# The first step of the expert loop, written out ahead of the loop in SyncE's program

## The chip, the cores and the metric

The kernel is one program on one core of a Trainium2 chip. Its five engines (TensorE or PE, VectorE or DVE, ScalarE or ACT, GpSimd or POOL, SyncE or SP) run their own instruction streams and meet at semaphores. SyncE computes nothing here: it issues nearly all transfers from HBM into SBUF. The metric is the device time of one execution, in microseconds (us), and its median over several runs.

## The reference

One denoising step of a small network: two layers over 128 context tokens and 128 latent tokens, width 1024, float32. Layer 0 mixes tokens by a two-way linear recurrence and a convolution, layer 1 by differential attention. After either mixer comes the part that the change touches, a mixture of experts on all 256 tokens:

```python
g_idx = jnp.argmax(g_logits, axis=-1)                      # one of 4 groups
e_in = jnp.take_along_axis(e_logits, g_idx[:, None, None], axis=1)[:, 0]
top_v, top_i = lax.top_k(e_in, TOP_K_INNER)                # 2 of its 8 experts
eid = g_idx[:, None] * EXPERTS_PER_GROUP + top_i
...
hid = jax.nn.silu(einsum('nd,edf->nef', hf, w_gate)) * einsum('nd,edf->nef', hf, w_up)
out = einsum('nef,efd->nd', hid * gates[..., None], w_down)
```

Each layer has 32 experts; an expert has 1024 x 256 gate and up weights and 256 x 1024 down weights. Which experts a token needs is known only after the router has run on the chip.

## The kernel before, in words

In each layer the router (PE and DVE) sorts the 512 pairs of token and expert by expert and cuts each expert's pairs into chunks of CH = 32 rows. The chunks are dealt to NC = 4 columns, one 32-wide strip of the PE array each, and the expert loop takes one chunk of every column per step. DVE writes the table of this into `meta`, a row of integers in SBUF: `meta[0]` is the number of steps (at most MAXS = 12), from M_EID on stand the expert numbers (four for each step), and from M_LOAD on four flags for each step, which say whether that column's expert is another one than in the step before. The flags of the first step are always 1. Then DVE raises the semaphore `meta0` (in layer 1 `meta1`; L1958), which SP, PE, ACT and DVE wait for.

SP then runs its own loop. It reads the number of steps into a register (L592). In each step it reads four expert numbers (L594) and four flags (L596), and then issues three sets of four transfers by L601: `gu0`, the first half of the gate and up weights of each column, `gu1`, the second half, and `down`. Each transfer is 128 partitions x 2048 floats, 1 MB, from an address that the expert number gives, into the buffer `EW` (program name `arena`), and it takes place only if its flag is 1. `EW` has one place for each column and part, so SP waits before each set until PE has done with it in the step before (`gu0_done`, `gu1_done`, `down`); PE raises all three once ahead of the loop, in its program before it waits for the last numbers of the table.

PE's loop does per step: the `gu0` matmuls (L1084, 32 of them), the `gu1` matmuls (L1084, 32 more), the gather of the next step's tokens (L1058), two transposes each at L1097 and L1100, the scatter of the previous step's result (L1069), and the `down` matmuls (L1112). The first gather (L1058) stands ahead of the loop; its result is copied into SBUF by ACT (L1395) and DVE (L2009), and the first `gu0` matmuls need these copies and the four `gu0` transfers. After the loop come two layer norms on DVE (the last at L1519 to L1545), the next layer, or the end.

Of the kernel before, what the change touches and what calls it, by code (L numbers as in the profile page):

```python
# [22 lines left out]
T = 128  # L23
NS = 2
# [11 lines left out]
NE = NG * EPG  # L36
FF = 256
CH = 32
NC = 4
MAXS = 12  # L40
GRID_W = 64
ROPE_BASE = 10000.0
LAM_INIT = 0.8 - 0.6 * float(np.exp(-0.3))
# [45 lines left out]
def rope_tables():  # L89
    nf = HD // 4  # L90
    inv = ROPE_BASE ** (-np.arange(nf, dtype=np.float64) / nf)
    tok = np.arange(T)
    pos = np.stack([tok // GRID_W, tok % GRID_W], 1)
    ang = pos[:, :, None] * inv[None, None, :]
# [79 lines left out]

M_EID, M_LOAD = 4, 4 + NC * MAXS
M_ALL = M_LOAD + NC * MAXS


def build(nc, a, o):
# [4 lines left out]
    def S(name):  # L184

        if name not in sems:
            sems[name] = ctx.enter_context(nc.semaphore(name))
        return sems[name]

    arena = ctx.enter_context(nc.sbuf_tensor("arena", [P, ARENA], F32))  # L190
    meta = ctx.enter_context(nc.sbuf_tensor("meta", [1, 1, M_ALL], I32))
# [3 lines left out]
    def region(n):  # L195
        at = top[0]
        top[0] += n
        assert top[0] <= ARENA, top[0]
        return at

    def view(at, n, pattern=None, **sizes):
        v = arena[:, at:at + n]
        return v.rearrange(pattern, **sizes) if pattern else v
# [16 lines left out]
    cond = view(region(KT * 32), KT * 32, "p (k n) -> p k n", k=KT)  # L220
# [7 lines left out]
    def sv(at, n, pattern=None, **sizes):  # L228
        assert at + n <= SCR, (at + n, SCR)
        return view(scr + at, n, pattern, **sizes)  # L230
# [20 lines left out]
    for c in range(6):  # L251
        n = min(4, 23 - 4 * c) * P
# [15 lines left out]
    for c in range(2):  # L268
        chunk(("out", 1, c), a["od_out_w"][c], 512, ("mix", 1, 1, c))
    at_chunk = {name: i for i, (name, *_) in enumerate(chunks)}  # L270
    ring_ld = [S(f"ring_loaded{i}") for i in range(3)]


    ASIDE = {("mod", 0, 3): 8192, ("evin", 0): 0, ("evin", 1): 4096}
    in_ring = [i for i, (name, *_) in enumerate(chunks) if name not in ASIDE]
    turn = {i: r for r, i in enumerate(in_ring)}

# [14 lines left out]
    def load_chunk(sp, i):  # L292
        name, src, cols, _ = chunks[i]
        if name in ASIDE:
            sp.dma_start(sv(PRE + ASIDE[name], 8 * cols), src).then_inc(S("loaded_" + "_".join(map(str, name))), 16)
            return
        r = turn[i]
        if r >= 3:
            BK.wait_filled(sp, chunks[in_ring[r - 3]][3])
        sp.dma_start(ring[:, r % 3, 0:8 * cols], src).then_inc(ring_ld[r % 3], 16)  # L300
# [213 lines left out]
    EW = sv(0, 4 * 6144, "p (b n) -> p b n", b=4)  # L514
# [21 lines left out]
    GU = [(0, 2048), (2048, 4096)]  # L536
    DN = (4096, 6144)
# [7 lines left out]
    def norm_no(l, w, s):  # L545
        return (l * 2 + w) * 2 + s
# [5 lines left out]
    def bias_dma(eng, n):  # L552

        l, c = MOD_ORDER[n]
        eng.dma_start(bias_at(n)[0:2, :], a["mod_b"][l:l + 1, c * 512:(c + 1) * 512].partition_broadcast(2))\
            .then_inc(S(f"ld_mbias{n % 3}" if n >= 4 else "ld_mbias_first"), 16)


    @block.sync
    def _(sp):  # L560
        sp.dma_start(condw[:, 32:48], a["cond"].rearrange("p k s -> p (k s)")).then_inc(S("ld_cond"), 16)
        load_chunk(sp, 0)
        sp.wait_ge(S("mbias_zero"), 2)
        for n in range(4):
            bias_dma(sp, n)
        sp.dma_start(cst, a["cst"]).then_inc(S("ld_cst"), 16)
        load_chunk(sp, 1)
        load_chunk(sp, 2)
        sp.dma_start(x[:, 0, :], a["x_prompt"]).then_inc(S("ld_x"), 16)
        sp.dma_start(x[:, 1, :], a["x_sample"]).then_inc(S("ld_x"), 16)  # L570
        load_chunk(sp, 3)
        sp.dma_start(vec, a["vec"]).then_inc(S("ld_vec"), 16)
        for i in range(4, 6):
            load_chunk(sp, i)
        sp.dma_start(wup, a["ev_w_up"]).then_inc(S("ld_up"), 16)
        sp.dma_start(aup, a["ev_a_up"]).then_inc(S("ld_up"), 16)
        sp.dma_start(gup, a["ev_g_up"]).then_inc(S("ld_up"), 16)
        for i in range(6, FIRST_OF_1 + 1):
            if i == 8:
                BK.wait_filled(sp, ("mod", 0, 3))  # L580
                sp.dma_start(S0, a["s0t"]).then_inc(S("ld_s0"), 16)
            load_chunk(sp, i)
        for l in range(2):

            BK.wait_filled(sp, ("mix", l, 1, 1))
            sp.dma_start(rw, a["r_w"][l].rearrange("p (k n) -> p k n", k=KT)).then_inc(S("ld_rw"), 16)

            sp.wait_ge(S("x_new"), norm_no(l, 0, 1) + 1)
            sp.wait_ge(S(f"meta{l}"), 1)
            if l == 1:  # L590
                sp.wait_ge(S("cache_out"), 32)
            steps = sp.value_load(meta[0:1, 0, 0:1], min_val=1, max_val=MAXS)  # L592
            with sp.Fori(0, steps) as it:
                expert = [sp.value_load(meta[0:1, 0, bass.ds(it * NC + (c + M_EID), 1)], min_val=0, max_val=NE - 1)  # L594
                          for c in range(NC)]
                fresh = [sp.value_load(meta[0:1, 0, bass.ds(it * NC + (c + M_LOAD), 1)], min_val=0, max_val=1)  # L596
                         for c in range(NC)]

                def load(part, lo, hi):
                    for c in range(NC):  # L600
                        sp.dma_start(EW[:, c, lo:hi],  # L601
                                     a["w_exp"][l, bass.ds(expert[c], 1), :, lo:hi].rearrange("e p n -> p (e n)"),
                                     cond=fresh[c]).then_inc(S(f"{part}_loaded{l}"), 16)

                for h, (lo, hi) in enumerate(GU):
                    sp.wait_ge(S(f"gu{h}_done{l}"), it + 1)
                    load(f"gu{h}", lo, hi)
                sp.wait_ge(S(f"down{l}"), it * 2 + 2)
                load("down", *DN)
            if l == 0:  # L610
                sp.wait_ge(S("x_new"), norm_no(0, 1, 1) + 1)
                sp.dma_start(CK, a["cache_k"]).then_inc(S("ld_cache"), 16)
                sp.dma_start(CV, a["cache_v"]).then_inc(S("ld_cache"), 16)
                for i in range(FIRST_OF_1 + 1, len(chunks)):
                    load_chunk(sp, i)
        for s in range(NS):
            sp.wait_ge(S("x_new"), norm_no(1, 1, s) + 1)
            sp.dma_start(o["y"][s], x[:, s, :]).then_inc(S("y_out"), 16)
        sp.wait_ge(S("y_out"), 32)
# [80 lines left out]
    def _(pe):  # L700
# [302 lines left out]
        def moe(l):  # L1003
# [71 lines left out]
            pe.wait_ge(S(f"meta{l}"), 1)  # L1075
            steps = pe.value_load(meta[0:1, 0, 0:1], min_val=1, max_val=MAXS)
            with pe.Fori(0, steps) as n:
# [127 lines left out]
    def _(act):  # L1205
# [169 lines left out]
        def moe(l):  # L1375
# [13 lines left out]
            act.wait_ge(S(f"meta{l}"), 1)  # L1389
            steps = act.value_load(meta[0:1, 0, 0:1], min_val=1, max_val=MAXS)  # L1390
            act.sem_inc(S(f"y_read{l}"), 1)
# [80 lines left out]
    def _(dve):  # L1472
# [386 lines left out]
        def moe(l):  # L1859
# [72 lines left out]
            own.link(TS(sc[:, 40:41], bank[:, 32:33], 1.0 / NC, None, ALU.mult))  # L1932
            own.link(TS(rv(R_KV, MAXS), cst[:, C_G4 + 12:C_G4 + 12 + MAXS], sc[:, 40:41], None, ALU.is_lt))
            own.link(V.tensor_reduce(sc[:, 48:49], rv(R_KV, MAXS), AX, ALU.add))
# [255 lines left out]
```

## Time and profile before

| | |
|---|---|
| runs | 1090.66, 1091.86, 1093.72 us; median 1091.86 us |
| profiled execution | 1089.75 us, of which the span of the profile is 1087.7 us |
| PE matmuls busy | 895.1 us (82% of the span) |
| DVE busy | 512.4 us (47%) |
| ACT busy | 171.2 us (16%) |
| mean granted TensorE clock | 0.887 of full speed |
| HBM to SBUF, queue of SP | 214.57 MB |

The profile gives the busy time of the engines, what each waited for, and a chain of work that ended last, followed back from the end of the program; what shortens a piece of that chain can shorten the program. Instructions of SP's own sequencer (reads of registers, arithmetic on them, issues of transfers) show as SPq. L592 is line 592 of the kernel before.

### The profile page before, as it was taken

How to read it: one execution, taken by the hardware profiler on the slowest of the kernel's cores; microseconds unless marked ns; L12 is line 12 of the kernel's file. 1: busy time of each engine (PE TensorE's matmuls, PEld its weight loads, DVE VectorE, ACT ScalarE, POOL GpSimd, SP SyncE). 2: the span in 40 equal slices, each digit the busy share in tenths (PEclk: the TensorE clock that was granted, in tenths of full speed). 3: DMA queues.
4: the chain of work that ended last, by engine and by line, in shares of the span. 5: the costliest groups of instructions: out<-in, count | busy, mean ns of one | idle time of the engine just before them, and what ended most of it. 6: DMA issues, size and time to landing. Idle time of an engine off the chain costs nothing.

```text
span 1087.7 us, 14397 instructions
## 1 busy us (share of the span) xinstructions
PE 895.1 (82%) x5288; PEld 545.2 (50%) x5288; DVE 512.4 (47%) x1212; ACT 171.2 (16%) x429; POOL 28.8 (3%) x56
## 2 busy tenths in 40 slices
PE   3899939999999997747998785999459658988983
PEld 1687826878778773533453332445334523533431
DVE  1248898676675755452242225110555532422335
ACT  0123211212111210200111002002330200110110
POOL 1000000000000000000000000000000000000000
PEclk9899959999998998867999897999569668999987
DMA  9901429555444401239689954642000267799980
GB/s 373 422 30 59 164 91 364 194 191 203 158 159 156 175 1 59 83 140 401 252 328 424 423 231 159 273 174 97 1 0 1 84 262 314 309 424 363 422 337 39
DMA packets 28778, 226.81 MB, mean 209 GB/s; under 512 B 4072, under 2 KB 4488, under 8 KB 7744
## 3 DMA queue, kind: packets, MB, share of 16 engines
q1 hardware_dynamic: 25216, 214.57, 49.3%
q0 software_dynamic: 3520, 11.66, 3.1%
q8 instruction: 28, 0.46, 0.2%
q14 instruction: 14, 0.11, 0.0%
HBM read 286.74 MB, written 2.39 MB: 266 GB/s over the span
## 4 chain that ended last, share of the span: by engine, by line
PE 62%; DMA 14%; DVE 13%; SPq 5%; issue 4%; ACT 2%; DVEq 0%; ACTq 0%
DMA arena<-in_w_exp 12%; PE ps L1128 8%; PE ps L1084 6%; PE ps L804 6%; PE ps L761 5%; PE ps L896 4%; PE ps L889 4%; PE ps L711 4%; PE ps L1069 4%; PE ps L1058 3%; PE ps L1112 3%; SPq L601 3%; PE ps L740 2%; DMA arena<-in_mod_w 2%; PE ps L731 1%
## 5 line engine op out<-in xcount | busy, mean ns | idle before, releaser
L1084 PE MATMUL ps<-arena 128*32 128x512 f32 x960 | 129.6, 693 | 56.2 <-DMA arena<-in_w_exp 56.1
L1084 PEld LDWEIGHTS ps<-arena 128*32 128x32 f32 x960 | 32.8, 125 | 149.3 <-issue 78.7
L2020 DVE TENSOR_SCALAR arena<-arena 128x256 f32<-128x256 f32 x15 | 4.4, 296 | 178.0 <-ACT arena L1400 178.0
L1128 PE MATMUL ps<-arena 128*128 128x512 f32 x192 | 85.1, 604 | 3.8 <-ACT arena L1222 3.8
L804 PE MATMUL ps<-arena 128*128 128x256 f32 x368 | 81.6, 380 | 2.3 <-ACT arena L1222 1.5
L1214 ACT ACTIVATE arena<-ps 128x512 f32<-128x512 f32 x74 | 44.0, 602 | 227.1 <-PE ps L889 135.2
L804 PEld LDWEIGHTS ps<-arena 128*128 128x128 f32 x368 | 69.0, 189 | 15.2 <-ACT arena L1222 1.9
L740 PE MATMUL ps<-arena 128*128 128x128 f32 x208 | 37.2, 336 | 40.0 <-DVE arena L2116 24.7
L1058 PEld LDWEIGHTS ps<-arena 128*128 128x128 f32 x544 | 62.1, 191 | 15.6 <-issue 13.3
L711 PE MATMUL ps<-arena 128*32 128x512 f32 x384 | 53.9, 667 | 18.7 <-DMA arena<-in_cst 12.8
L1058 PE MATMUL ps<-arena 128*128 128x128 f32 x544 | 65.1, 277 | 0.6 <-DVE arena L1988 0.6
L1069 PE MATMUL ps<-arena 128*128 128x512 f32 x136 | 61.4, 593 | 1.8 <-DVE arena L2033 1.8
L1128 PEld LDWEIGHTS ps<-arena 128*128 128x128 f32 x192 | 36.9, 193 | 50.9 <-issue 46.5
L761 PE MATMUL ps<-arena 128*128 128x512 f32 x128 | 59.7, 622 | 1.6 <-ACT arena L148 1.6
L896 PE MATMUL ps<-arena 128*128 128x192 f32 x320 | 60.0, 330 | 0.0
L889 PE MATMUL ps<-arena 128*128 128x128 f32 x384 | 56.8, 293 | 2.3 <-issue 2.3
L889 PEld LDWEIGHTS ps<-arena 128*128 128x128 f32 x384 | 49.0, 199 | 16.5 <-issue 14.9
L740 PEld LDWEIGHTS ps<-arena 128*128 128x128 f32 x208 | 31.1, 178 | 50.4 <-DVE arena L2116 28.0
L1112 PE MATMUL ps<-arena 128*32 128x512 f32 x480 | 54.6, 595 | 0.0
L896 PEld LDWEIGHTS ps<-arena 128*128 128x128 f32 x320 | 52.5, 194 | 0.0
L1811 DVE COPY arena<-ps 128x256 f32<-128x256 f32 x80 | 33.9, 424 | 37.3 <-PE ps L896 37.3
L1721 DVE SCALAR_TENSOR_TENSOR arena<-arena 128x256 f32<-128x256 f32 x120 | 51.4, 479 | 0.0
(296 smaller groups left out, 1049.4 us busy)
## 6 DMA issues: line engine op xcount, KB each, us to landing
arena<-in_w_exp SPq DMA_DIRECT2D x180, 1024.0 KB
arena<-in_mod_w SPq DMA_DIRECT2D x24, 2048.0 KB, 8.2
arena<-in_od_in_w SPq DMA_DIRECT2D x6, 2048.0 KB, 8.0
arena<-in_ev_in_w SPq DMA_DIRECT2D x5, 2048.0 KB, 28.0
arena<-in_ev_out_w SPq DMA_DIRECT2D x2, 2048.0 KB, 8.6
arena<-gate_rows POOLq DMA_DIRECT2D x8, 512.0 KB, 4.5
arena<-in_ln POOLq DMA_DIRECT2D x4, 1024.0 KB, 4.9
arena<-in_od_out_w SPq DMA_DIRECT2D x2, 2048.0 KB, 8.1
```

The costliest lines, as they stand in the source:

```text
L711: mm = pe.matmul(bank[q:q + 32, :], cond[:, k, :], w[:, k, :], start=(k < 4), stop=(k >= 4), skip_group_check=True)
L740: mm = pe.transpose(bank[:, n * P:(n + 1) * P], t, ident)
L761: mm = pe.matmul(BK.bank(key), hT[:, k, s * T:(s + 1) * T], slot(("out", l, n))[:, k, :], start=(k == 0), stop=(k == KT - 1))
L804: mm = pe.matmul(bank[:, n * 256:n * 256 + 256], slot(("evin", i // 4))[:, k, (i % 4) * P:(i % 4 + 1) * P], hT[:, k, :], start=(k == 0), s ...
L889: mm = pe.matmul(BK.bank(key)[:, i * P:(i + 1) * P], now[:, i, 0:P], lt[i], start=True, stop=True)
L896: mm = pe.matmul(BK.bank(key)[:, (i % 2) * 192:(i % 2) * 192 + 192], lt[i], now[:, i, :], start=True, stop=True)
L1058: mm = pe.matmul(ps[:, 4 + k // 4, (k % 4) * P:(k % 4 + 1) * P], hb[:, s, k * P:(k + 1) * P], sel[:, s, :], start=(s == 0), stop=(s == 1))
L1069: mm = pe.matmul(ps[:, 2 * s + half, :], tG[:, s * P:(s + 1) * P], ysb[:, half * 512:(half + 1) * 512], start=False, stop=last, skip_group ...
L1084: mm = pe.matmul(ps[32 * c:32 * c + 32, 6, :], xg[:, k, 32 * c:32 * c + 32], EW[:, c, k * 512:(k + 1) * 512], start=(k == 0), stop=(k == K ...
L1112: mm = pe.matmul(ps[32 * c:32 * c + 32, 4 + half, :], tH[:, f * P + 32 * c:f * P + 32 * c + 32], w, start=(f == 0), stop=(f == 1), skip_gr ...
L1128: mm = pe.matmul(BK.bank(key), hT[:, k, s * T:(s + 1) * T], slot(("odin", c))[:, k, :], start=(k == 0), stop=(k == KT - 1))
L1721: ins = STT(out, src, w, out, ALU.mult, ALU.add)
```

## The change

SP's first step is taken out of its loop. It waits for `gu1_done` and `down` once; then it reads the number of one expert and issues that column's `gu0` transfer, four times over, and issues the `gu1` and `down` sets behind them. These twelve transfers have no flag, and the four flags of the first step are not read. Then it reads the number of steps and runs the loop from step 1 on, which is as it was. The number of steps is declared to be at least MINS = 4 in SP's program. It is so for both layers. No other engine's program is changed.

```diff
+MINS = 2 * NS * T // (CH * NC)
...
-            steps = sp.value_load(meta[0:1, 0, 0:1], min_val=1, max_val=MAXS)
-            with sp.Fori(0, steps) as it:
+            def load(part, lo, hi, c, expert, **when):
+                sp.dma_start(EW[:, c, lo:hi], a["w_exp"][l, bass.ds(expert, 1), :, lo:hi].rearrange("e p n -> p (e n)"),
+                             **when).then_inc(S(f"{part}_loaded{l}"), 16)
+
+            sp.wait_ge(S(f"gu1_done{l}"), 1)
+            sp.wait_ge(S(f"down{l}"), 2)
+            first = []
+            for c in range(NC):
+                first.append(sp.value_load(meta[0:1, 0, M_EID + c:M_EID + c + 1], min_val=0, max_val=NE - 1))
+                load("gu0", *GU[0], c, first[c])
+            for c in range(NC):
+                load("gu1", *GU[1], c, first[c])
+            for c in range(NC):
+                load("down", *DN, c, first[c])
+            steps = sp.value_load(meta[0:1, 0, 0:1], min_val=MINS, max_val=MAXS)
+            with sp.Fori(1, steps) as it:
                 expert = [sp.value_load(meta[0:1, 0, bass.ds(it * NC + (c + M_EID), 1)], min_val=0, max_val=NE - 1)
                           for c in range(NC)]
                 fresh = [sp.value_load(meta[0:1, 0, bass.ds(it * NC + (c + M_LOAD), 1)], min_val=0, max_val=1)
                          for c in range(NC)]
 
-                def load(part, lo, hi):
+                for h in range(2):
+                    sp.wait_ge(S(f"gu{h}_done{l}"), it + 1)
                     for c in range(NC):
-                        sp.dma_start(EW[:, c, lo:hi],
-                                     a["w_exp"][l, bass.ds(expert[c], 1), :, lo:hi].rearrange("e p n -> p (e n)"),
-                                     cond=fresh[c]).then_inc(S(f"{part}_loaded{l}"), 16)
-
-                for h, (lo, hi) in enumerate(GU):
-                    sp.wait_ge(S(f"gu{h}_done{l}"), it + 1)
-                    load(f"gu{h}", lo, hi)
+                        load(f"gu{h}", *GU[h], c, expert[c], cond=fresh[c])
                 sp.wait_ge(S(f"down{l}"), it * 2 + 2)
-                load("down", *DN)
+                for c in range(NC):
+                    load("down", *DN, c, expert[c], cond=fresh[c])
```

The first place is where SP comes from the wait for `meta0` in layer 0. TENSOR_LOAD is a read of a number from SBUF, and ISA stands for arithmetic on registers. Before, the rows from there on are these:

```order
L592 TENSOR_LOAD meta [waits meta0,x_new]
L592 ISA x2
L593 UNCONDITIONAL_BRANCH
L593 ISA
L594 TENSOR_LOAD meta
L594 ISA x3
```

Three more reads by L594 and four by L596 follow, and the first transfer stands behind them:

```order
L596 TENSOR_LOAD meta
L596 ISA x2
L606 REGISTER_ALU
L601 ISA [waits gu0_done0]
L601 DMA arena<-in_w_exp 128x2048
```

Now the same place has one read ahead of the first transfer (L601 is now the read of an expert number and L594 the transfer):

```order
L601 TENSOR_LOAD meta [waits gu1_done0,down0,meta0,x_new]
L601 ISA x2
L594 ISA
L594 DMA arena<-in_w_exp 128x2048
L601 TENSOR_LOAD meta
```

Of the nine reads that stood ahead of the first transfer one is left: three expert numbers are now read between the first four transfers, the number of steps behind the twelfth, and the four flags of the first step not at all. The second place is SP's way from the last transfer of the first step into the loop, which is new:

```order
L594 DMA arena<-in_w_exp 128x2048
L607 TENSOR_LOAD meta
L607 ISA x2
L608 UNCONDITIONAL_BRANCH
L608 ISA
L609 TENSOR_LOAD meta
```

The read of the number of steps now stands there, behind twelve transfers. The rows of the loop's body, eight reads and twelve transfers, are the same as before but for their line numbers, and layer 1 has the same change.

## Rows read from the trace of the kernel before

**Rows 1.** The page's chain that ended last, shares of the span by engine and line

```profile
PE 62%; DMA 14%; DVE 13%; SPq 5%; issue 4%; ACT 2%; DVEq 0%; ACTq 0%
```

**Rows 2.** The chain, layer 0, in order: start us, us, what

```profile
470.95 0.07 DVE arena L1958
471.09 0.46 SPq L592
...
471.95 0.07 SPq L593
...
475.61 0.43 issue
...
477.67 0.16 SPq L601
...
477.93 0.36 SPq L601
```

**Rows 3.** The chain, layer 1, same columns

```profile
872.99 0.28 SPq L592
...
873.64 0.07 SPq L593
...
878.86 0.17 SPq L601
...
879.14 0.34 SPq L601
...
881.05 0.33 SPq L601
```

**Rows 4.** The timeline, both layers: start us, us, engine, line, [idle before <-releaser]

```profile
481.37 0.69 DVE L2009 COPY arena<-ps 128x512 f32<-128x512 f32 x1 [2.41 <-PE ps L1058]
...
492.27 6.23 PE L1084 MATMUL ps<-arena 128*32 128x512 f32 x32 [11.04 <-DMA arena<-in_w_exp]
...
882.89 0.69 DVE L2009 COPY arena<-ps 128x512 f32<-128x512 f32 x1 [2.26 <-PE ps L1058]
...
891.75 6.17 PE L1084 MATMUL ps<-arena 128*32 128x512 f32 x32 [8.99 <-DMA arena<-in_w_exp]
```

**Rows 5.** Stretches: length, busy of five engines, granted clock, DMA share, GB/s

```profile
474.00:476.00 2.00, 2.00 (x3) 0.67 (x2) 0.92 (x2) 0.00 (x0) 0.00 (x0) 0.50 0.00 0
...
478.00:480.00 2.00, 2.00 (x20) 2.00 (x20) 0.92 (x4) 0.52 (x1) 0.00 (x0) 1.00 0.53 106
...
482.00:484.00 2.00, 0.00 (x0) 0.00 (x0) 1.06 (x5) 0.00 (x0) 0.00 (x0) 0.97 0.90 311
...
488.00:490.00 2.00, 0.00 (x0) 0.00 (x0) 0.00 (x0) 0.00 (x0) 0.00 (x0) 0.50 0.99 418
...
880.00:882.00 2.00, 2.00 (x20) 2.00 (x19) 0.60 (x3) 0.60 (x1) 0.00 (x0) 1.00 0.97 283
882.00:884.00 2.00, 0.76 (x7) 0.57 (x6) 1.08 (x3) 0.00 (x0) 0.00 (x0) 1.00 1.02 426
```

**Rows 6.** The chain behind the first expert matmuls, both layers

```profile
483.62 18.55 DMA arena<-in_w_exp
502.21 6.38 PE ps L1084 x32
508.59 3.77 PE ps L1058 x32
...
519.81 6.88 PE ps L1084 x64
...
901.71 6.31 PE ps L1084 x32
...
919.24 6.88 PE ps L1084 x62
```

**Rows 7.** SP's loop ends, L593, layer 0, then layer 1: ns min/median/max, first and last start

```profile
L593 SPq ALU_OP  x7: 33/33/33, 487.1 to 628.4; - x7
...
L593 SPq ALU_OP  x8: 33/33/41, 887.7 to 1043.4; - x8
```

## The prediction

> **What bounds the kernel now.** I read the shares of the chain first [rows 1]. PE holds 62% of it, but 14% is waiting for transfers and 5% is SP's own sequencer, so what SP does one instruction at a time can set the end. The chain in order of time shows where. When DVE has raised the flag at 470.95 us, nothing else is on the chain but SP's reads until its first transfer at 477.93 [rows 2]; in layer 1 the same stretch runs from 872.99 to 879.14 [rows 3]. Then I asked the timeline what waits for these transfers. PE stands idle 11.04 us in layer 0 and 8.99 us in layer 1 ahead of its first expert matmuls, released by a transfer both times [rows 4]. The stretches show that the DMA engines have nothing to do meanwhile (share 0.00 at 474 to 476) and run at 418 GB/s once they are going [rows 5]. So both layers have a stretch in which DMA waits for SP and PE waits for DMA. Behind it the chain waits for the `gu1` transfers (until 502.21) and then goes from one PE line to the next through the first two steps [rows 6]. Nothing in it is fixed in time: each piece is released by the one before, so a start that is earlier by some time moves the rest by as much.
>
> **The change part by part.** *The reads ahead of the first transfer.* Before, SP reads the number of steps from 471.09 to 471.95, then enters the loop and reads four experts and four flags until the address arithmetic of the first transfer at 477.67. What stands between 471.95 and 477.67, 5.72 us, is gone from ahead of the first transfer, for the first expert number takes the place of the number of steps: same kind of read, two register instructions behind it, as the order shows [rows 2]. In layer 1 it is 878.86 less 873.64, 5.22 us [rows 3]. The two layers differ by 0.5 us mostly because of a hole of 0.43 us at 475.61 that layer 1 lacks; I take each as it was. Sum 10.94 us.
>
> *Two waits added ahead* (`gu1_done` and `down`, where `gu0_done` alone stood later). In PE's program they are raised ahead of PE's own wait for the table, so they are up when SP comes; what is left is the instruction. The trace has no wait that is satisfied at once with its gaps measured apart; the step from DVE's flag to the first read, 470.95 to 471.09, is 0.14 us and holds such a wait [rows 2]. I take 0.1 us a layer, with ends 0 and 0.28. Minus 0.2 us in all.
>
> *Three reads between the first four transfers.* They delay the second to the fourth transfer. A read with its register instructions took 0.86 us in layer 0 (471.09 to 471.95) and 0.65 us in layer 1, so three take 2.6 or 2.0 us. From SP's first issue to the fourth it took 1.9 us in layer 1 [rows 3]; it will be some 4. A transfer of 1 MB takes 2.5 us at 418 GB/s [rows 5], so the DMA engines come to the fourth only 7.5 us behind the start. I take nothing; the upper end is the three reads in full, 4.6 us for both layers.
>
> *The flags.* The first step's transfers took place before as well, since its flags are 1. No byte is saved. A transfer without a flag has as many instructions as one with it.
>
> *The number of steps, and the loop's first reads, now behind twelve issues.* When does SP come to the second step? Twelve issues took 9.2 us in layer 0 (477.93 to 487.1) and 8.6 us in layer 1 [rows 7]. To that come three reads (2.6, then 2.0), the number of steps (0.9, then 0.7) and the entry with eight reads (5.7, then 5.2). From a first transfer at 472.3 that is 490.7 in layer 0, and from 874.0 it is 890.5 in layer 1. What it must not miss is the end of the first `gu0` matmuls, now 492.27 + 6.23 = 498.5, then 492.9; in layer 1 891.75 + 6.17 = 897.9, then 892.8 [rows 4]. So the cover is 2.2 and 2.3 us: nothing is paid, and if the cover were gone, SP's next set would start late by what is missing, which costs only once its data is late for the second step (rival D).
>
> *PE's side of the wait.* The copy of the gathered tokens ends at 481.37 + 0.69 = 482.1 and 883.6. The transfers would let PE start at 492.27 less 5.6 = 486.7, and 891.75 less 5.1 = 886.6 [rows 4]. The copies are earlier by 4.6 and 3.0 us, so DMA is still what ends the wait, and the whole gain arrives. Were it not so, the gain would stop at the copy.
>
> **Sum:** 10.94 - 0.2 = 10.7 us, 5.6 in layer 0 and 5.1 in layer 1. Against the profiled execution, 1089.75, that is 1079.0 us; that execution lies 2.1 us under the median of the runs, 1091.86, and from the median it is **1081.2 us**.
>
> The read of a number takes 0.46 us in layer 0 and 0.28 in layer 1 [rows 2, 3]. The Trainium skill (DMA: Bandwidth & Descriptors, Latency and other measured facts) gives a floor of about 600 ns for it. By that floor the one read that is left would be longer by 0.14 and 0.32 us and the gain 10.2 us in place of 10.7; the trace has it shorter, and the sum goes by the trace.
>
> **How fast the transfers get going** is the largest unknown of size. From SP's first issue to PE's first expert matmul it is 14.3 us in layer 0 and 12.6 us in layer 1 for the same 4 MB [rows 2 to 4], because in layer 0 the engines are counted as busy at 0.90 yet move only 311 GB/s at 482 to 484, where layer 1 moves 426 two to four microseconds after its first transfer [rows 5]. I see no cause in the trace. If it hangs on the moment and not on the kernel, layer 0 may gain 1.7 us more, or layer 1 1.7 us less: 9.0 to 12.4 us in place of 10.7.
>
> **The clock of PE.** It was granted half speed (1.2 GHz) while PE was idle ahead of the expert matmuls [rows 5], and the first `gu1` matmuls took 6.38 and 6.31 us where 64 matmuls took 6.88 at 2.4 GHz [rows 6], which is 3.44 for 32. The idle time gets shorter, and if that kept the clock up, the chain would gain up to 2.9 us a layer more. Against it: a wait ahead of `gu1` remains, and a `gu0` done sooner makes that one longer. I take no gain.
>
> **The rivals.** *A. More than the sum:* the clock comes back earlier in both layers; 10.7 + 5.8 = 16.5 us at most, 1075.4. *B. Hidden anyway:* something other than SP's issue decides when the data lands, so that the stretch is filled by a slow start of DMA; 1091.9. For it speaks that layer 0 needs 1.7 us more for the same bytes; against it that the DMA engines stand at share 0.00 all the way until SP issues. The Trainium skill (DMA: Bandwidth & Descriptors, Issuing engines are not separate DMA queues) says that the sequencer's time to start a transfer is usually small beside the transfer. It would make this rival the likely one; here eight reads stand ahead of the start, 5 to 6 us of them, and no transfer runs beside them. *C. Part of it is given back:* layer 1 starts slowly too and the waits and reads cost their upper ends (0.6 and 4.6 us, of which I took 0.2): 10.7 - 1.7 - 5.0 = 4.0 us, 1087.9. *D. Slower:* SP's program has become longer, and SP must now get at the loop's instructions while 12 MB of transfers are under way, where before it entered the loop with DMA idle. If it stood still there until these twelve have landed (12.6 MB at 418 GB/s is 30 us, so until some 504 in layer 0 and 906 in layer 1), then reads took 6 us and the next `gu0` 12.6 us, it would land at 522 and 924. PE wants it at 519.81 - 5.6 = 514.2 and 919.24 - 5.1 = 914.1 [rows 6]. It costs 8 and 10 us, the whole is 7 us slower, 1099. It decides once the stop is beyond 16 us: about 11 us are covered (490.7 against 514.2 less 12.6), and 5.4 a layer are the gain. The only hole seen is 0.43 us [rows 2].
>
> **How the numbers follow.** About 0.3%, 3.3 us, is what can be told from no change. The forecast, a gain of 8.5 to 13 us, gets 0.66; A (13 to 17 us) 0.12; C (3.3 to 8.5 us) 0.13; B 0.06; D 0.03. The likeliest case's own range is 1078.9 to 1083.4. With half of A and half of C taken in, and for the 3 us by which the runs of before differ among themselves, the range is 1076.5 to 1085.5. Faster by over 0.3%: 0.91; within: 0.06; slower: 0.03.
>
> **What would show it.** In the trace of after, SP's first expert transfer comes 1.0 to 1.2 us behind the flag (before 7.0), PE's idle time ahead of the first expert matmuls is 5 to 6 us in layer 0 and 3.5 to 4 in layer 1, both still released by a transfer, and the distance from the first transfer to the first matmul stays between 12.6 and 14.3 us. SP's first transfer of the second step comes right behind the end of the first `gu0` matmuls and not behind SP's reads. The prediction is wrong if DMA starts early and the data lands as before, if PE is released by the copies, or if SP comes late to the second step.

## The result, and the profile after

| | before | changed |
|---|---|---|
| runs of the first comparison | 1091.26 us median of 4 (1089.07 to 1093.72) | 1076.37 us median of 4 (1069.36 to 1081.01) |
| ratio, 95% interval | | 0.9857 (0.9819 to 0.9895) |
| first repeat | 1091.93 (25 runs) | 1081.37 (6 runs), ratio 0.9885 (0.9847 to 0.9923) |
| second repeat | 1090.3 (11 runs) | 1079.05 (6 runs), ratio 0.9899 (0.9858 to 0.9940) |
| profiled execution | 1089.75 us, span 1087.7 | 1081.01 us, span 1078.9 |

The change makes the kernel faster by 1.0 to 1.4%. The first median, 1076.4 us, lies 4.8 us under the forecast of 1081.2 and just outside its range (from 1076.5); both repeats lie inside it, 0.2 us over and 2.2 us under the forecast.

The chain of the changed kernel, layer 0 (start us, us, what; L1969 is DVE's flag, L601 the read of an expert number, L594 a transfer of experts). It answers to [rows 2]:

```profile
474.72 0.07 DVE arena L1969
...
474.86 0.47 SPq L601
...
475.84 0.35 SPq L594
...
476.23 0.28 SPq L601
...
476.95 0.34 SPq L594
...
478.05 0.33 SPq L594
...
479.14 0.34 SPq L594
...
479.56 0.43 issue
```

And layer 1, which answers to [rows 3]:

```profile
869.82 0.07 DVE arena L1969
...
869.96 0.28 SPq L601
...
870.72 0.34 SPq L594
...
874.45 0.33 SPq L594
```

The first transfer now comes 1.12 and 0.90 us behind the flag, where it came 6.98 and 6.28 us behind it: 5.86 + 5.38 = 11.2 us. The hole of 0.43 us that stood among the reads of layer 0 is still there, at 479.56, but now behind the first four transfers, where it costs nothing. Layer 1, which had none before, now has one of 0.36 us at 872.96, between its second and third transfer.

The timeline, PE's first expert matmuls (L1095) and DVE's copy (L2020), both layers, as in [rows 4]:

```profile
485.16 0.69 DVE L2020 COPY arena<-ps 128x512 f32<-128x512 f32 x1 [2.42 <-PE ps L1069]
489.47 6.12 PE L1095 MATMUL ps<-arena 128*32 128x512 f32 x32 [4.45 <-DMA arena<-in_w_exp]
...
879.86 0.69 DVE L2020 COPY arena<-ps 128x512 f32<-128x512 f32 x1 [2.27 <-PE ps L1069]
884.25 5.01 PE L1095 MATMUL ps<-arena 128*32 128x512 f32 x32 [4.52 <-DMA arena<-in_w_exp]
894.19 5.16 PE L1095 MATMUL ps<-arena 128*32 128x512 f32 x32 [4.93 <-DMA arena<-in_w_exp]
```

PE's idle time has gone from 11.04 to 4.45 us and from 8.99 to 4.52, and a transfer still ends it, 3.6 and 3.7 us after the copy. Behind it the chain has the pieces of [rows 6]:

```profile
482.03 17.34 DMA arena<-in_w_exp
499.37 0.04 issue
499.41 6.27 PE ps L1095 x32
505.68 3.77 PE ps L1069 x32
...
516.89 3.42 PE ps L1095 x29
```

One way of adding up the profile serves for all that follows. The span is cut into five parts: up to DVE's flag in layer 0; from there to the end of the first `gu1` matmuls (stretch 0); on to the flag in layer 1 (middle); to the end of the first `gu1` matmuls there (stretch 1); and the tail. Each number is a difference of starts and ends in the timeline. For before, stretch 0 is 502.21 + 6.38 - 470.95 = 37.64 us. The flag of layer 1 before is this row of its chain:

```profile
872.86 0.07 DVE arena L1958
```

| profile | up to flag 0 | stretch 0 | middle | stretch 1 | tail |
|---|---|---|---|---|---|
| before | 470.95 | 37.64 | 364.27 | 35.16 | 179.68 |
| changed | 474.72 | 30.96 | 364.14 | 29.53 | 179.55 |
| changed, repeat 1 | 473.17 | 30.99 | 364.14 | 31.82 | 180.58 |
| changed, repeat 2 | 475.83 | 31.53 | 364.12 | 31.83 | 179.49 |

Middle and tail are the same to about 1 us, as the argument needs that a start earlier by some time moves the rest by as much. The two stretches sum to 72.8 us before and to 60.5, 62.8 and 63.4 after, on average 62.2: 10.6 us less, against 10.7 forecast. By layer the forecast is less close: layer 0 gained 6.1 to 6.7 us against 5.6, layer 1 gained 5.6, 3.3 and 3.3 against 5.1. What does not fit is the first 470 us, which in these four profiles differ by 4.9 us though their programs are equal.

### The profile page after: what moved, and what is told of

Same layout as the page of the kernel before. It is cut to its first block, busy times and chain, and to the rows that moved or that the text cites. A ratio compares the mean times of both kernels' runs of the same rounds, so it can differ in the third digit from the quotient of the medians.

```text
span 1078.9 us, 14351 instructions
## 1 busy us (share of the span) xinstructions
PE 895.7 (83%) x5288; PEld 548.5 (51%) x5288; DVE 512.4 (47%) x1212; ACT 170.8 (16%) x429; POOL 28.8 (3%) x56
## 4 chain that ended last, share of the span: by engine, by line
PE 62%; DMA 14%; DVE 13%; SPq 5%; issue 3%; ACT 2%; DVEq 0%; ACTq 0%
DMA arena<-in_w_exp 12%; PE ps L1139 8%; PE ps L1095 6%; PE ps L815 6%; PE ps L772 6%; PE ps L907 5%; PE ps L900 4%; PE ps L722 4%; PE ps L1080 4%; PE ps L1069 3%; PE ps L1123 3%; SPq L594 3%; DMA arena<-in_mod_w 2%; PE ps L751 2%; ACT arena L1233 1%
## 5 line engine op out<-in xcount | busy, mean ns | idle before, releaser
L1095 PE MATMUL ps<-arena 128*32 128x512 f32 x960 | 126.7, 679 | 46.5 <-DMA arena<-in_w_exp 46.3
L1095 PEld LDWEIGHTS ps<-arena 128*32 128x32 f32 x960 | 32.5, 123 | 137.4 <-issue 76.3
L815 PEld LDWEIGHTS ps<-arena 128*128 128x128 f32 x368 | 70.4, 193 | 15.6 <-ACT arena L1233 1.9
L1069 PEld LDWEIGHTS ps<-arena 128*128 128x128 f32 x544 | 62.1, 192 | 15.1 <-issue 12.9
L722 PE MATMUL ps<-arena 128*32 128x512 f32 x384 | 53.5, 662 | 18.9 <-DMA arena<-in_cst 12.8
L1139 PEld LDWEIGHTS ps<-arena 128*128 128x128 f32 x192 | 37.0, 194 | 50.9 <-issue 46.5
L900 PEld LDWEIGHTS ps<-arena 128*128 128x128 f32 x384 | 49.8, 202 | 15.8 <-issue 13.3
L751 PEld LDWEIGHTS ps<-arena 128*128 128x128 f32 x208 | 30.6, 176 | 50.4 <-DVE arena L2127 28.1
L1123 PE MATMUL ps<-arena 128*32 128x512 f32 x480 | 54.6, 595 | 0.0
L907 PEld LDWEIGHTS ps<-arena 128*128 128x128 f32 x320 | 54.5, 200 | 0.0
```

The costliest lines, as they stand in the source:

```text
L722: mm = pe.matmul(bank[q:q + 32, :], cond[:, k, :], w[:, k, :], start=(k < 4), stop=(k >= 4), skip_group_check=True)
L751: mm = pe.transpose(bank[:, n * P:(n + 1) * P], t, ident)
L815: mm = pe.matmul(bank[:, n * 256:n * 256 + 256], slot(("evin", i // 4))[:, k, (i % 4) * P:(i % 4 + 1) * P], hT[:, k, :], start=(k == 0), s ...
L900: mm = pe.matmul(BK.bank(key)[:, i * P:(i + 1) * P], now[:, i, 0:P], lt[i], start=True, stop=True)
L907: mm = pe.matmul(BK.bank(key)[:, (i % 2) * 192:(i % 2) * 192 + 192], lt[i], now[:, i, :], start=True, stop=True)
L1069: mm = pe.matmul(ps[:, 4 + k // 4, (k % 4) * P:(k % 4 + 1) * P], hb[:, s, k * P:(k + 1) * P], sel[:, s, :], start=(s == 0), stop=(s == 1))
```

## The experiments

All are edits of the changed kernel. *first* is its list of expert numbers of the first step. The arrival times at the first transfer are from the timelines: start of SP's first transfer less start of DVE's flag.

**The changed kernel again, twice.** No edit.

> The changed kernel itself, timed against the kernel before in five rounds, and profiled a second time. Theory 1, SP's reads: all of the gain lies between DVE's flag and SP's first expert transfer. In the trace the first transfer comes 1.1 us behind the flag in layer 0 and 0.9 in layer 1, where it was 7.0 and 6.3, so 11.3 us, and the time is 1079 to 1081 if the run before is at 1091 (ratio 0.989 to 0.990). Theory 2, the clock adds: PE is granted its full clock for longer behind the shorter waits, some 3 to 4 us more than the reads account for, ratio 0.985 to 0.987, and the stretch from the flag to the end of the first gu1 matmuls is shorter by over 12 us in sum. Theory 3, what the profiled pair shows outside the two stretches (3.8 us in the first 470 us, where the programs are equal) is chance: it has another size or sign in this profile.

> The changed kernel once more, five rounds, for its size. If the first four runs (median 1076.4) were a chance draw of a wide scatter: ratio between 0.987 and 0.991, and in the trace the two stretches from DVE's flag to the end of the first gu1 matmuls sum to 60 to 63 us (72.8 before), with the time ahead of the first flag somewhere in 470 to 478 us. If the change gives more than its stretches: ratio 0.986 or lower and a middle part (between the two stretches) under 363.5 us.

Ratios 0.9885 and 0.9899, medians 1081.37 and 1079.05 us. The first transfer came 1.12 and 0.90 us behind the flag in all three profiles. The stretches are in the table above. Theory 1 holds for the place of the gain: the repeats' stretches are shorter by 10.0 and 9.4 us, where theory 2 asked for over 12 (the first profile had 12.3). The 63.4 us of the second repeat lie a little above its expected 60 to 63; its middle, 364.12, is not the shorter one that its rival asked for. Theory 3 holds as well: the time up to the first flag was 474.7, 473.2 and 475.8 us in the three profiles of this kernel, and in all twelve profiles of the study it lies between 470.1 and 477.5 without any order that follows the edits. The view by stretches says what differs, here for the shortest and the longest of them, `four_first` and `nine_first`, whose programs are equal up to there:

```profile
0.00:470.09 470.09, 404.52 (x2547) 309.34 (x2547) 293.74 (x674) 89.02 (x209) 22.98 (x45) 0.92 0.44 167
```

```profile
0.00:477.46 477.46, 414.40 (x2547) 314.39 (x2547) 293.71 (x673) 89.17 (x209) 23.04 (x45) 0.90 0.43 164
```

The columns are length, then busy time of PE, PE's weight loads, DVE, ACT and POOL with their instructions, the granted clock, DMA share and GB/s. The same 2547 matmuls keep PE busy for 9.9 us more at a mean clock of 0.90 than at 0.92, and DVE, ACT and DMA do the same work in the same time. So the scatter in this part is PE's clock: how long it is granted 1.2 GHz in a stretch differs from one execution to the next. The runs without a profile agree. Over the 48 runs of the kernel before that the three later comparisons hold, the time falls by about 8.5 us for each 0.01 of mean granted clock (correlation -0.84), and over the 16 runs of the changed kernel by 9.5 us (-0.80). The slowest of the 48 had the lowest clock (0.879, 1099.4 us), and the fastest of the 16 the highest (0.902, 1069.4 us).

**All nine reads ahead of the first transfer again** (`nine_first`), the step still outside the loop, with its flags.

```diff
-            first = []
-            for c in range(NC):
-                first.append(sp.value_load(meta[..., M_EID + c:M_EID + c + 1], ...))
-                load("gu0", *GU[0], c, first[c])
...
-            steps = sp.value_load(meta[0:1, 0, 0:1], ...)
+            steps = sp.value_load(meta[0:1, 0, 0:1], ...)
+            first = [sp.value_load(meta[..., M_EID + c:M_EID + c + 1], ...) for c in range(NC)]
+            flag = [sp.value_load(meta[..., M_LOAD + c:M_LOAD + c + 1], ...) for c in range(NC)]
+            for c in range(NC):
+                load("gu0", *GU[0], c, first[c], cond=flag[c])       # and so for gu1 and down
```

> The first step stays ahead of the loop, but all nine reads stand in front of its first transfer as before (the number of steps, four experts, four flags), and the transfers have their flags. Theory 1: the nine reads at 0.5 to 0.65 us put the first transfer at 5 to 6 us behind the flag; only the address arithmetic of the reads and the loop entry are saved, so it is faster than the kernel before by 1 to 3 us and slower than the changed one by 8 to 10 (ratio 0.997 to 0.999). The rival, that a step ahead of the loop or a transfer without a flag is what gained: the ratio stays at 0.986 to 0.990.

Ratio 0.9963 (0.9936 to 0.9990), 1088.2 us. Its chain shows the reads back on it (L599 to L601):

```profile
477.46 0.07 DVE arena L1969
...
477.61 0.47 SPq L599
...
478.42 0.27 SPq L600
...
480.63 0.27 SPq L601
...
482.56 0.44 issue
...
483.56 0.36 SPq L594
```

The first transfer came 6.10 and 5.81 us behind the flag, the stretches sum to 69.0 us. Most of the gain is gone though the step is still outside the loop, so it was the reads. At the first transfer 1.35 us are left of it: the loop entry and the address arithmetic of reads with a counter, less a hole of 0.36 us that this kernel has among its reads in layer 1. The time came out a little better than expected, 3.7 us under before and 7 to 9 over the changed kernel. The stretches are 3.8 us shorter than before; beyond the 1.35 us that is a faster start of the transfers (1.2 us) and first `gu1` matmuls that took 5.05 us in layer 1 in place of 6.31.

**The flags kept** (`flags_kept`): each of the four columns reads its flag behind its expert number, and all twelve transfers have theirs.

```diff
                 first.append(sp.value_load(meta[..., M_EID + c:M_EID + c + 1], ...))
-                load("gu0", *GU[0], c, first[c])
+                flag.append(sp.value_load(meta[..., M_LOAD + c:M_LOAD + c + 1], ...))
+                load("gu0", *GU[0], c, first[c], cond=flag[c])
```

> As the changed kernel, but each of the first four columns has its flag read behind its expert number, and all twelve transfers have their flags. Theory 1: one read more ahead of the first transfer, 0.5 us a layer, so 1.0 to 1.3 us slower than the changed kernel; the first four transfers are 1.7 us apart, still under the 2.5 us that one takes to move. The rival, that the transfers without flags start or move faster: the distance from the first transfer to the first expert matmul grows again to 12.6 to 14.3 us, and the loss is 3 us or more.

Ratio 0.9916 (0.9892 to 0.9939), 1082.9 us. First transfer at 1.80 and 1.96 us, 0.7 and 1.1 us later than in the changed kernel; from there to the first expert matmul 14.56 and 13.45 us, about what the changed kernel's profiles show (13.5 to 14.8). The stretches sum to 64.3 us, 2.0 more than the changed kernel's mean. So a transfer without a flag is not seen to get going faster; the flags cost their reads, some 1.7 us together.

**Four reads, then four transfers** (`four_first`).

```diff
-            first = []
+            first = [sp.value_load(meta[..., M_EID + c:M_EID + c + 1], ...) for c in range(NC)]
             for c in range(NC):
-                first.append(sp.value_load(meta[..., M_EID + c:M_EID + c + 1], ...))
                 load("gu0", *GU[0], c, first[c])
```

> As the changed kernel, but the four expert numbers are read in one go ahead of the first transfer, which the four transfers then follow as fast as SP can issue. Theory 1: the first transfer comes 1.6 to 2.0 us later in each layer, so it is 3.2 to 4 us slower than the changed kernel. If transfers that follow each other fast reach full rate sooner than ones that are 1.1 us apart, a part of it comes back: the distance from the first transfer to the first gu1 matmul is then under the 23.5 us that the changed kernel's trace shows in both layers.

Ratio 0.9912 (0.9878 to 0.9946), 1082.0 us. The first transfer came 2.78 and 2.58 us behind the flag, 3.3 us later in sum than in the changed kernel. But to the first expert matmul it was then 13.64 and 12.74 us only, and to the first `gu1` matmul 23.5 and 22.7, where the changed kernel's three profiles have 24.1 and 24.3 on average. The stretches sum to 63.3 us, 1.1 us more than the changed kernel's mean and not the 3.2 to 4 of theory 1. What gives two thirds back shows in the rates. These are the first 10 us behind the first transfer in layer 1, in `four_first`:

```profile
868.17:878.17 10.00, 6.68 (x38) 4.55 (x36) 5.71 (x19) 0.60 (x1) 0.00 (x0) 0.95 0.91 353
```

in `before`, whose four follow each other 0.64 us apart in this layer:

```profile
879.14:889.14 10.00, 3.62 (x32) 3.43 (x31) 3.15 (x11) 0.60 (x1) 0.00 (x0) 0.88 0.92 360
```

and in the changed kernel, with two stretches of it:

```profile
870.72:872.72 2.00, 2.00 (x4) 0.86 (x3) 1.72 (x9) 0.00 (x0) 0.00 (x0) 0.50 0.54 94
...
874.72:876.72 2.00, 1.39 (x9) 0.83 (x8) 1.85 (x9) 0.00 (x0) 0.00 (x0) 1.00 1.00 365
...
870.72:880.72 10.00, 8.39 (x40) 5.24 (x38) 6.32 (x24) 0.60 (x1) 0.00 (x0) 0.87 0.90 329
```

The first 2 us are alike in all three (94 to 111 GB/s). The difference lies at 4 to 8 us behind the first transfer, where the DMA engines count as busy in all (share 0.90 to 1.03). They move 418 to 434 GB/s there in the three profiles without reads between the transfers, and 287 to 377 in seven of the nine with reads between them; `both` (381 and 418) and `warm` (422 and 397) lie higher. Over 10 us it is 329 against 353 and 360 GB/s in the rows shown, so about 0.3 MB or 0.7 us. PE does nearly the same work in `four_first` as in the changed kernel (38 and 40 matmuls in these 10 us), so it is not PE's work beside them.

Layer 0 of the kernel before looks like an exception, for it has no reads between its transfers and yet starts slowly. Its chain shows that its transfers do not follow each other closely either, since the issues of the second and the third took long:

```profile
478.58 0.99 SPq L601
479.85 0.74 SPq L601
```

From the first to the fourth transfer it takes 2.9 us there, where layer 1 takes 1.9. Sorted by that distance, all 24 bursts (twelve profiles, two layers) fall into two groups. Five have it at 1.6 to 2.0 us (`nine_first` and `four_first` in both layers, before in layer 1) and move 353 to 360 GB/s over their first 10 us; nineteen have it at 2.9 us or more and move 308 to 351. To the first expert matmul the five take 12.3 to 12.7 us in layer 1 and 13.5 and 13.6 in layer 0, the others 13.1 to 14.8 in layer 1 and 13.6 to 14.9 in layer 0. On average the others are 1.3 us later in layer 1 and 0.9 in layer 0. That the distance is the cause is argued and not shown: it was changed together with the moment of the first transfer, and a slow issue may be a sign of slow DMA engines as well as its cause.

**More reads behind the twelve transfers** (`late_reads`: 8, `late_many`: 32).

The edit of `late_many`:

```diff
+            for c in range(8 * NC):
+                sp.value_load(meta[0:1, 0, M_EID + c:M_EID + c + 1], min_val=0, max_val=NE - 1)
             with sp.Fori(1, steps) as it:
```

> As the changed kernel, with eight reads more (not used) behind the read of the number of steps, 4.4 to 5 us a layer. In the changed kernel's trace SP is ready for its second step 5.3 us before the first gu0 matmuls end in layer 0 and 2.8 us in layer 1. Theory 1, the prediction's cover: the reads eat it, SP's transfers for the second step come up to 2 us late in layer 1, and nothing is lost, since their data is wanted only some 11 us later than the latest issue in time; the same time as the changed kernel within 1 us. The rival, that the length of SP's program or its arrival at the loop matters by itself: slower by the added time, 5 to 10 us.

> As the changed kernel, with 32 reads more behind the read of the number of steps, 17 to 19 us a layer. Theory 1: SP comes some 12 to 16 us late to its second step; the data of the second step is then late by 1 to 8 us a layer, so 3 to 14 us slower than the changed kernel in sum, and PE has an idle time ahead of the second step's gu0 matmuls, released by a transfer, which it does not have in the changed kernel. If the slack of about 11 us that the prediction worked out is larger than thought, nothing is lost.

`late_reads`: ratio 0.9912 (0.9877 to 0.9947), 1081.1 us, as expected no loss to be seen (stretches 63.2 us, middle 364.1). `late_many`: 0.9916 (0.9885 to 0.9947), 1080.4 us, and here 3 to 14 us of loss were expected. SP came to its second step 12 and 15 us late (the first `gu0` matmuls ended at 492.3 and 885.3, SP was ready at 504.5 and 900.5). PE's timeline for the second step, first layer 0, then layer 1:

```profile
513.05 7.06 PE L1097 MATMUL ps<-arena 128*32 128x512 f32 x64
...
906.80 3.65 PE L1097 MATMUL ps<-arena 128*32 128x512 f32 x32 [0.22 <-DMA arena<-in_w_exp]
910.84 1.50 PE L1097 MATMUL ps<-arena 128*32 128x512 f32 x12 [0.40 <-DMA arena<-in_w_exp]
```

PE waits for the second step's data not at all in layer 0 and 0.6 us in layer 1. The middle part, which holds the second step of layer 0, is 364.0 us, as in the changed kernel, and the tail 178.9. The reason is in the durations of SP's transfers of that step (least, median, longest in ns):

```profile
L594 SPq DMA_DIRECT2D arena<-in_w_exp x12: 73/73/348, 504.8 to 514.6; - x12
```

An issue that moves data takes 333 ns or more; most of these take 73. Their flags are 0: in the second step most columns keep their expert, so there is far less than 12 MB to move and far more slack than the 11 us that were worked out from four transfers of a set.

**PE kept busy in the wait** (`warm`): five matmuls between the first gather and PE's loop.

```diff
             gather(0)
+            for n in range(5):
+                pe.matmul(ps[:, 7, :], ident, cst[:, 0:512], start=True, stop=True, skip_group_check=True)
```

> As the changed kernel, with five matmuls of 128x512 more on PE (into a PSUM bank that the first step does not use yet, result not used) between the first gather and the expert loop, about 4.3 us at 2.4 GHz. They fill the idle time ahead of the first gu0 matmuls. The theory that the clock sets a part of the gain: with the clock kept up the gu0 matmuls take 3.4 us in place of 5 to 6. By the prediction's reasoning the wait ahead of gu1 grows by the same 2 to 3 us, since the gu1 data sets its end, and the time stays that of the changed kernel within 1.5 us (longer wait, clock falls again). The rival: the clock stays up through gu1 as well, 2 to 3 us a layer faster.

Its timeline in layer 0, where L1087 is the added matmuls:

```profile
480.32 4.46 PE L1087 MATMUL ps<-arena 128*128 128x512 f32 x10
486.15 3.65 PE L1097 MATMUL ps<-arena 128*32 128x512 f32 x32 [1.37 <-DMA arena<-in_w_exp]
496.08 5.67 PE L1097 MATMUL ps<-arena 128*32 128x512 f32 x32 [6.28 <-DMA arena<-in_w_exp]
```

The first set takes 3.65 us in place of 6.12, the wait behind it is 6.28 us in place of 3.8, and the `gu1` set is slower again, 5.67 us. In layer 1 the first set follows the added matmuls without idle time (they end at 879.6), so it may have started some 0.3 us late there. The stretches sum to 60.8 us, within the changed kernel's 60.5 to 63.4. The ratio, 0.9875 (0.9839 to 0.9911), is no better than the changed kernel's within its interval. So no worth is seen in the clock of the first set, as the prediction argued. A `gu1` set at the full clock was not reached in it, and so its worth was not tried.

**The same idea for the later steps** (`rotated`, and `both`): a step's eight reads, and those of the step before once more for its `down` set, stand ahead of the wait for `down`. In `both` DVE also raises a semaphore right with the row of expert numbers, for SP's first transfers.

```diff
...
+            with sp.Fori(2, steps) as it:
+                old, was = read(it - 1, M_EID, NE - 1), read(it - 1, M_LOAD, 1)
+                expert, fresh = read(it, M_EID, NE - 1), read(it, M_LOAD, 1)
+                sp.wait_ge(S(f"down{l}"), it * 2)
+                for c in range(NC):
+                    load("down", *DN, c, old[c], cond=was[c])
+                for h in range(2):
+                    sp.wait_ge(S(f"gu{h}_done{l}"), it + 1)
+                    for c in range(NC):
+                        load(f"gu{h}", *GU[h], c, expert[c], cond=fresh[c])
...
-            own.inc(V.tensor_copy(meta[0:1, 0, M_EID:M_EID + NC * MAXS], eid))
+            sig(V.tensor_copy(meta[0:1, 0, M_EID:M_EID + NC * MAXS], eid), f"eid{l}")
```

> As the changed kernel, and the same idea for the later steps: the reads of a step's four experts and four flags (and those of the step before once more, for its down set) now stand behind its predecessor's gu1 set and ahead of the wait for down, where SP waits for PE for some 11 us. In the kernel before, these eight reads are on the chain once in layer 0 (558 to 564) and three times in layer 1 (939.6, 981, 1024), some 6 us each. Theory 1, reads of SP between a release and the transfer that PE will wait for are paid in full only where DMA is idle: up to 24 us if all four come out, but PE waits for that set's data only 3.8 us or less plus the slower clock behind it, so 3.8 to 5.7 us each, 15 to 23 us faster than the changed kernel. The rival, that the bytes bind in these steps: under 5 us.

> The rotated kernel, and in addition DVE raises a semaphore of its own right with the row of expert numbers, which SP waits for ahead of its first transfers; the flag of the whole table SP now waits for only ahead of the number of steps. In the chain of before 0.5 us lie between that row (472.15 in layer 1 for 872.15) and the flag (872.86), so the first transfer comes 0.4 to 0.6 us earlier in each layer, some 1 us in all, and the rotated loop gives its 4 us in layer 1's tail once more: ratio 0.983 to 0.987, the fastest kernel of the study. If the rotated kernel's ratio of 0.987 was chance: 0.988 or more, and a tail as long as the changed kernel's (179 to 181 us).

`rotated`: ratio 0.9869 (0.9833 to 0.9906), 1076.3 us; `both`: 0.9882 (0.9837 to 0.9926), 1077.3 us. 15 to 23 us beyond the changed kernel were expected of `rotated` and a ratio of 0.983 to 0.987 of `both`; neither can be told from the changed kernel. The reads did leave the chain. In the changed kernel it goes through eight of them at this place in layer 1 (two of the eight are shown):

```profile
930.28 0.34 SPq L594
931.02 0.28 SPq L609
...
935.55 0.26 SPq L611
936.43 0.34 SPq L594
...
940.29 14.00 DMA arena<-in_w_exp
954.33 5.34 PE ps L1095 x32
```

and in `rotated` through none:

```profile
933.94 0.08 SPq L594
...
934.31 0.33 SPq L594
...
934.92 15.84 DMA arena<-in_w_exp
950.80 3.65 PE ps L1106 x32
```

but the piece of DMA is still there, and longer. PE's wait behind it went from 3.80 to 3.12 us. In `rotated` PE still waits for `gu1` in three steps of layer 0 (3.8, 6.3 and 3.8 us) as in the changed kernel, which fits the expectation's rival, that the bytes set the distance. The tail was 175.2 us in `rotated` but 179.1 in `both`, and 175.7 in `warm`, which leaves the loop as it was, so the first is not shown to be the reads. The signal of its own did what it should: in `both` the first transfer comes 0.54 and 0.30 us behind the flag of the table, 0.6 us earlier in each layer; 1.2 us in all is less than these timings can tell.

## Why the prediction was right in its steps and missed with its range

**Which reads are on the path: right.** The first transfer came 5.86 and 5.38 us earlier against 5.6 and 5.1. With the reads put back it went to 6.10 and 5.81 us behind the flag, and most of the gain with it. PE's idle time came out at 4.5 to 5.4 us in layer 0, about as forecast, but at 4.5 to 5.8 in layer 1, where 3.5 to 4 were forecast.

**The added waits: over-sized.** I took 0.1 us a layer. From flag to first read it is 0.14 us before and after in both layers, so they cost nothing. Likewise the read was shorter than the floor of the Trainium skill (DMA: Bandwidth & Descriptors, Latency and other measured facts) in every profile shown here, 0.47 and 0.28 us. The prediction's 10.2 us by that floor were worked out wrongly besides: it lengthened the one read that is left and not the eight that are gone, with which the gain by the Trainium skill's figure would come out larger and not smaller.

**Three reads between the first four transfers, and the start of the transfers: mis-sized.** I took nothing, with 2.0 to 2.6 us a layer as the end. The fourth transfer was indeed in time, but the start to the first expert matmul took 13.5 to 14.8 us where 12.6 to 14.3 was expected: in layer 0 14.15 on average against 14.34 before, in layer 1 14.33 against 12.61. So the slow start that the prediction held possible for layer 1 came in full, and the same size that layer 0 might have won did not. What I found no cause for has a sign in the trace, the two long issues of layer 0 (0.99 and 0.74 us), by which its four transfers were spread out before the change too. By `four_first` the reads between the transfers cost 0.5 us in layer 0 and 1.6 in layer 1, from one profile; why the DMA engines are slower while they count as busy stays open.

**The sum: right by luck.** The first transfers brought 11.2 us, the start of the transfers took 1.5 back (0.2 won in layer 0, 1.7 lost in layer 1), and the first `gu1` matmuls were 0.9 us shorter, which the sum had at nothing: 10.6 us, against 10.7 forecast. Single terms were off by up to 1.7 us and the sum by 0.1.

**The cover of SP's way into the loop: too small on the safe side.** SP was ready 5.3 and 2.8 us ahead of the end of the first `gu0` matmuls, against 2.2 and 2.3, so the stop that rival D supposed did not come. D had a wrong price as well: it counted four moving transfers in a set, where the flags let few move, and a delay of 12 to 15 us cost 0.6 us and not the 1 to 8 a layer that I expected of `late_many`.

**Rivals A to C.** A, the clock: the first `gu1` matmuls took 5.2 to 6.3 us in the changed kernel's profiles against 6.38 and 6.31, and with PE kept busy ahead of the `gu0` set nothing was gained. The mean of the six is 5.92, so up to 0.9 us of the gain in sum may be the clock; that was not shown apart from chance. B (hidden anyway) is excluded by the idle times. The Trainium skill's rule beside it (DMA: Bandwidth & Descriptors, Issuing engines are not separate DMA queues), that the sequencer's time to start a transfer is usually small beside the transfer, agrees with the trace for the issue alone, 0.33 to 0.36 us for most beside some 2.5 us for 1 MB. What was not small is the eight reads ahead of the issue, of which the rule says nothing. In the later steps, taking reads off SP's way gave nothing that can be told. C had the right mechanism at a part of its price: its 1.7 us for a slow start in layer 1 came, its further 5.0 us for waits and reads did not.

**The range: the step that failed.** It was widened "for the 3 us by which the runs of before differ among themselves". That was three runs, and this term is the one that failed. 48 further runs of the kernel before spread over 16.7 us (1082.7 to 1099.4), and the 16 of the changed kernel over 15.5 us (1069.4 to 1084.8), median 1079.2. Drawn from these runs at random, a median of four is over 3 us off in about one draw of six before and one of nine after. The first comparison, 0.1 us outside the range, was nearly such a draw, 2.9 us under the median of all 16. The sign and the place of the gain were right, and the size within what the runs can tell; the scatter of a median was mis-sized, and its cause, PE's clock also in stretches that the change does not touch, had not been looked for.

Open is a rest of some 2 us: the three ratios average 0.988, a gain of 13 us with an uncertainty of about 2.4, while the stretches of the profiles give 10.6, and for before there is one profile only. Chance in that one profile, or a little of the clock in the parts outside the stretches, could each fill it.

## What to carry to other kernels

Where a loop's transfers depend on numbers in SBUF, look at what the issuing engine reads between the release and the first transfer: at the start, with DMA idle and the others waiting, every read is paid in full, and it is enough to read what the first transfer needs. A long way from the first to the fourth transfer was followed by a slower burst here, so what is won by reading late is partly given back. The same reads in the later steps, with bytes in flight, were worth nothing that could be measured, though the chain of waits went through them: a piece of the chain is only worth what the next constraint behind it leaves. And before a range is given, the scatter of runs has to be known from more than three of them; cutting the span at fixed events and comparing part by part gave gains of 9.4 to 12.3 us from single profiles, where medians of four to six runs gave 10.6 to 14.9.

## What the runs showed of the hardware

- Four transfers of 1 MB that are issued within 1.6 to 2.0 us (five bursts) moved 353 to 360 GB/s over the burst's first 10 us, four that were spread over 2.9 us or more (nineteen bursts) 308 to 351, though 1 MB takes some 2.5 us to move at 418 GB/s, and at about the same DMA share (0.91 to 0.92 against 0.87 to 0.91).
- A transfer whose flag is 0 takes SP's queue 73 ns as a rule, one that moves data 333 ns or more.
- In layer 0 the hole of 0.43 us in SP's stream stays about as far behind the start of its reads, whatever instruction stands there: at 475.61 before, at 479.56 in the changed kernel and at 482.56 in `nine_first`, 4.5 to 5.0 us behind the first read. In layer 1 it is 0.36 us and moves: none before, 3.0 us behind the first read in the changed kernel, 1.1 us in `nine_first`. Its cause was not looked into.
- PE's time for the same 2547 matmuls varied between 404.5 and 414.4 us from one execution to another with the granted clock, without any change of the program in that stretch.
